# Strassen's scheme for 24 of the 32 up slabs of a decoder layer, with relu squared moved to ScalarE

## The chip, the cores and the metric

The kernel runs on one core of a Trainium2 chip. The metric is the device time of one launch in microseconds, as the median of several runs.

## What is computed

One layer of a decoder for 1056 tokens (1024 of a prompt, 32 of eight sample requests) of 1024 features: a gated convolution and pooling block, a cross attention, and a feed-forward block, each followed by a layer norm. The change lies in the last block:

```python
f = jnp.square(jax.nn.relu(x @ w1 + b1)) @ w2 + b2     # w1: 1024 x 4096, w2: 4096 x 1024
x = layer_norm(DN_ALPHA * x + f, ln3_g, ln3_b)
```

All arithmetic is in float32. For the products on TensorE each operand is kept as two parts in the matmul's own format, a high part (the rounded value) and a low part (the rest), and each product is three matmuls: high by high, high by low and low by high, all summed in PSUM.

## The kernel before, in words

Everything is held with the features on the partitions: x is 8 blocks of 128 features by 1056 tokens, as `xh` (high) and `xl` (low). A matmul writes at most a bank of PSUM, so the tokens are cut into three chunks of 384, 384 and 288 columns. The weights come as slabs of 128 partitions by 1024 columns (512 KB), one slab for one block of 128 outputs, into the two slots of `raw`.

The feed-forward block has two stages. In the **up stage** ("W1") 32 slabs of w1 are run through as plain products. GpSimd splits a slab into `wh` and `wl` (two instructions, lines 473 and 475), TensorE makes 3 chunks of 8 x 3 matmuls, ScalarE reads each chunk with bias and relu (line 1807), VectorE squares it (line 2435), and SyncE writes the finished block to `hidden` in DRAM. Slab n takes the slots of slab n-2, so its split begins when slab n-2 is done. Between the squares VectorE sets up the residual's sums in `acc` (lines 2439, 2440).

In the **down stage** ("ST") 24 of the 32 blocks of hidden values are taken by Strassen's scheme already: six groups of four blocks, each with four units of seven products of quarter size. The seven forms (sums of quarters of the hidden values, over 528 columns, half the tokens) are made by VectorE (line 2366), cast by ScalarE (line 1783) and given their low parts by VectorE and GpSimd (lines 2372, 752). The forms of the weights are made likewise for each unit: sums by VectorE (line 2388), casts by ScalarE (line 1796), low parts by GpSimd (line 759). A product is 12 matmuls of 264 columns in one of four pairs of banks, and VectorE adds it to its sums from PSUM (line 2404). The last 8 blocks are kept with both parts in DRAM and are done as plain slabs at the end ("W2").

Each engine works through a queue of its own, in the order in which the program text issues it; semaphores tie the queues together. The order is written out by hand. The first pair of up slabs is done chunk by chunk while the norm before it still writes x.

Of the kernel before, what the change touches and what calls it, by code (L numbers as in the profile page):

```python
# [6 lines left out]
P = 128  # L7
# [76 lines left out]
LATE = LAST - NU  # L84
# [27 lines left out]
STAGES += [("W1", times(16, SIX), (2, 5)), ("ST", {}, ()), ("W2", *LINEAR), ("C3", LN_MEAN, ()), ("T3", SIX, ())]  # L112
# [9 lines left out]
def decoder_step(nc, hidden, xT, memT, slabs, pool_w, params, consts, conv_state, pool_state, dec_kv,  # L122
# [76 lines left out]
    unit_high = at("unit_high", [P, 2, T], f32r, O_Q + 28 * HT * 4)  # L199
    small = at("small", [P, 80], f32, O_SMALL)  # L200
# [86 lines left out]

    def units_out(j):

        return 16 * (j // 2 + 1) + 16 * max(0, (j - KEPT) // 2 + 1)  # L290

    def squared(j):

        return 3 * j + max(0, j - KEPT)
# [8 lines left out]
    def form_order(i, G):  # L303

        by_dve = i in BY_DVE_FORMS
        order = BY_DVE_FORMS if by_dve else BY_POOL_FORMS
        return sem("form_low_dve" if by_dve else "form_low_pool"), len(order) * G + order.index(i) + 1
# [6 lines left out]
    def _(sp):  # L314
# [66 lines left out]
        def hidden_out(j):  # L381

            p = j % 2
            sp.wait_ge(sem("square"), squared(j + 1))
            block = relu[:, p, :] if j < KEPT else relu_low[:, p, :].bitcast(f32)
            sp.dma_start(hidden[:, j, :], block).then_inc(sem(f"hidden_out{p}"), 16)
            if j >= KEPT:
                sp.dma_start(hidden[:, j + NB, :], unit_high[:, p, :].bitcast(f32)).then_inc(sem(f"hidden_out{p}"), 16)

        def forms_in(G):  # L390

            b = G % 2
            if G == 0:
                for p in range(2):
                    sp.wait_ge(sem(f"hidden_out{p}"), 32)
            elif G == 1:
                sp.wait_ge(used, S_ST)
                sp.wait_ge(sem("acc_set"), NB)
                for p in range(2):
                    sp.wait_ge(sem(f"hidden_out{p}"), 64)  # L400
            else:
                sp.wait_ge(sem("st_done"), 7 * UNITS * (G - 1))
# [9 lines left out]
        for j in range(UP):  # L412
            if j < UP - 2:
                load_next(S_FF + 4 + j)
            hidden_out(j)
            if j == 9:
                forms_in(0)
        for U in range(NU):
            sp.wait_ge(sem("w_form_low"), 7 * U + 6)
            sp.wait_ge(sem("weight_sums"), 4 * (U + 1))  # L420
# [3 lines left out]
            if U >= NU - UNITS:  # L424
                if U == NU - UNITS:
                    sp.wait_ge(sem("st_done"), 7 * (NU - UNITS))
# [31 lines left out]
    def _(pool):  # L458
# [287 lines left out]
        split(S_FF + 3, 1, S_FF // 2 + 1, MEM_SLABS, freed=S_XO + 8)  # L746
        def form_low(G, i):

            f = forms_full[G % 2][:, i]
            pool.wait_ge(sem("form_sums"), 4 * (G + 1))  # L750
            pool.wait_ge(sem("form_high"), 7 * G + FORM_HIGHS.index(i) + 1)
# [3 lines left out]
        def w_form_low(U, i):  # L755

            f = 7 * U + i
            pool.wait_ge(sem("w_form_high"), f + 1)
# [3 lines left out]
        splits(S_FF + 4, S_FF + 18)  # L762
        form_low(0, 0)
        form_low(0, 4)
        splits(S_FF + 18, S_FF + 20)
        form_low(0, 5)
        form_low(0, 6)
        splits(S_FF + 20, S_ST)
# [32 lines left out]
    def _(pe):  # L801
# [465 lines left out]
        pairs("W1", S_FF, 1, UP // 2, x_parts)  # L1267

        def unit_product(U, i):
# [4 lines left out]
            pe.wait_ge(sem("w_form_low"), f + 1)  # L1274
# [81 lines left out]
    def _(act):  # L1356
# [419 lines left out]
        def form_high(G, *which):  # L1776

            for i in which:
                if i in (0, 5, 6):
                    act.wait_ge(sem("forms_in"), 64 * (G + 1))  # L1780
                else:
                    act.wait_ge(sem("form_sums"), 4 * G + {2: 1, 3: 2, 1: 3, 4: 4}[i])
                act.copy(forms_high[G % 2][:, i], forms_full[G % 2][:, i]).then_inc(sem("form_high"), 1)

        def w_form_high(U, i):

            f = 7 * U + i
            if f < 8:
                act.wait_ge(used, S_ST - 1 if f < 4 else S_ST)
            else:  # L1790
                act.wait_ge(sem("st_done"), f - 7)
            if i in (0, 4, 5):
                act.wait_ge(*unit_raw(U))
            else:
                act.wait_ge(sem("weight_sums"), 4 * U + {2: 1, 3: 2, 1: 3, 6: 4}[i])
            act.copy(wh_forms[:, f % 8, :], weight_source(U, i)).then_inc(sem("w_form_high"), 1)  # L1796

        for j in range(UP):
            p = j % 2
            if j == UP - 1:  # L1800
                for i in range(4):
                    w_form_high(0, i)
            for c, (a, z) in enumerate(CHUNKS):
                b = slab_arrived(act, "W1", S_FF + j, p, c, j // 2)
                if c == 0 and j >= 2:
                    act.wait_ge(sem(f"hidden_out{p}"), units_out(j - 2))
                act.activation(relu[:, p, a:z], ps[b][:, 0:z - a], ACT.Relu, bias=col("b1", j)).then_inc(free[b], 1)  # L1807
            if j == 14:
                form_high(0, *FORM_HIGHS)
            if j >= KEPT:  # L1810
                act.wait_ge(sem("square"), squared(j) + 3)
                act.copy(unit_high[:, p, :], relu[:, p, :]).then_inc(sem("unit_high"), 1)
# [9 lines left out]
        def late_w_high(j):  # L1822
# [3 lines left out]
            act.wait_ge(sem("st_done"), 7 * NU if j else 7 * NU - 4)  # L1826
# [55 lines left out]
    def _(dve):  # L1882
# [473 lines left out]
        def form_sums(G, *which):  # L2356
# [3 lines left out]
            for i in which:  # L2360
# [3 lines left out]
                else:  # L2364
                    dve.wait_ge(sem("form_sums"), 4 * G + {3: 1, 1: 2, 4: 3}[i])
                tt(f[:, i], f[:, x], f[:, y], op).then_inc(sem("form_sums"), 1)  # L2366

        def form_low(G, i):

            dve.wait_ge(sem("form_sums"), 4 * (G + 1))  # L2370
            dve.wait_ge(sem("form_high"), 7 * G + FORM_HIGHS.index(i) + 1)
# [3 lines left out]
        def unit_weight_sums(U, *which):  # L2375
# [3 lines left out]
            for k in which:  # L2379
                if k:  # L2380
                    dve.wait_ge(sem("weight_sums"), 4 * U + k)
                else:
                    dve.wait_ge(*unit_raw(U))
                    if U > 1:
                        dve.wait_ge(sem("w_form_low"), 7 * (U - 1))
# [4 lines left out]
        def add_product(U, i):  # L2390
# [4 lines left out]
            dve.wait_ge(sem("st_done"), 7 * U + i + 1)  # L2395
            out, y = by_banks(target), pair(7 * U + i)
            if i == 1 and U in (0, 2):
                dve.wait_ge(sem(f"hidden_out{U // 2}"), units_out(UP - 1))
# [32 lines left out]
        for j in range(UP):  # L2431
# [181 lines left out]
```

## Time and profile before

| what | us |
|---|---|
| median of 3 runs | 1381.05 |
| lowest, highest | 1379.62, 1382.85 |
| the profiled execution | 1379.41 |
| its span, first to last instruction | 1377.6 |

The up stage ends at about 1010 us of the span, the down stage with its 168 products at about 1266 us. Times in the rows below are microseconds from the span's start. The profile is of one execution. Busy time is the time in which an engine has an instruction in work; matmuls are pipelined, so the durations of single matmuls overlap and their rate has to be read from a count in a stretch.

### The profile page before, as it was taken

The numbers are of one execution on the slowest core, as the hardware profiler recorded it, in microseconds if no ns is written. First come the engines' busy times: TensorE is split into PE (matmuls) and PEld (weight loads), VectorE is DVE, ScalarE is ACT, GpSimd is POOL, SyncE is SP. The second block draws the span as 40 slices with busy tenths as digits, with TensorE's granted clock in tenths as the row PEclk, the third lists the DMA queues.
The fourth block names the chain that finished last, engine by engine and source line by source line (L and its number), as shares of the span: only waits on it lengthen the run. The fifth ranks groups of instructions, "written<-read, shape, count | busy, mean of one in ns | idle before, by whom it ended". The sixth has DMA issues, their size and how long they took to land.

```text
span 1377.6 us, 21845 instructions
## 1 busy us (share of the span) xinstructions
PE 1326.0 (96%) x8744; PEld 1279.3 (93%) x8744; DVE 882.5 (64%) x1034; ACT 431.9 (31%) x821; POOL 783.7 (57%) x576
## 2 busy tenths in 40 slices
PE   6999999999999999999999999999999999989995
PEld 6999988788899978889999999999999999989995
DVE  5899994456612762387664246324469998897767
ACT  4223442245612441145211131112243444422233
POOL 3476987544933714629433337333359999994522
PEclk9999999989999999999999999999999999999998
DMA  8222452110020266201233433333343133346112
GB/s 257 69 51 45 126 162 78 31 46 1 32 61 31 76 234 239 80 16 46 79 93 93 156 93 93 93 93 140 140 162 109 58 110 125 110 158 206 57 47 81
DMA packets 59018, 136.91 MB, mean 99 GB/s; under 512 B 21568, under 2 KB 27968, under 8 KB 56512
## 3 DMA queue, kind: packets, MB, share of 16 engines
q1 hardware_dynamic: 49184, 132.99, 29.7%
q10 hardware_dynamic: 9760, 2.93, 0.9%
q8 instruction: 47, 0.77, 0.2%
q14 instruction: 27, 0.22, 0.1%
HBM read 107.02 MB, written 28.88 MB: 99 GB/s over the span
## 4 chain that ended last, share of the span: by engine, by line
PE 62%; DVE 27%; issue 3%; POOL 3%; DMA 2%; ACT 2%; SPq 0%; DVEq 0%; ACTq 0%; POOLq 0%
PE bank L809 20%; PE bank L810 19%; PE bank L811 19%; DVE bank L1901 11%; DVE ffn_sum L2404 2%; POOL w_low L759 2%; DVE form_low L2372 1%; DVE weight_sums L2388 1%; DVE product_sums L2404 1%; DMA form_full<-hidden 1%; DVE bank L2028 1%; DVE x_full L2018 1%; DVE x_full L2035 1%; DVE form_full L2366 1%; ACT x_full L1613 1%
## 5 line engine op out<-in xcount | busy, mean ns | idle before, releaser
L809 PE MATMUL bank<-x_high,w_high 128*128 128x384 f32 (+1 forms) x1200 | 391.0, 326 | 14.5 <-POOL w_low L475 11.3
L810 PE MATMUL bank<-x_low,w_high 128*128 128x384 f32 (+1 forms) x1200 | 388.3, 324 | 0.0
L811 PE MATMUL bank<-x_high,w_low 128*128 128x384 f32 (+1 forms) x1200 | 387.6, 323 | 0.0
L809 PEld LDWEIGHTS bank<-x_high,w_high 128*128 128x128 f32 x1200 | 226.0, 188 | 17.0 <-POOL w_low L475 10.1
L473 POOL TENSOR_TENSOR w_high<-w_raw,ones 128x1024 fp32r<-128x1024 f32 x48 | 92.0, 1916 | 240.4 <-issue 128.9
L811 PEld LDWEIGHTS bank<-x_high,w_low 128*128 128x128 f32 x1200 | 226.1, 188 | 0.0
L810 PEld LDWEIGHTS bank<-x_low,w_high 128*128 128x128 f32 x1200 | 226.1, 188 | 0.0
L2435 DVE TENSOR_TENSOR relu<-relu 128x384 f32<-128x384 f32 (+1 forms) x96 | 96.6, 1010 | 187.6 <-ACT relu L1807 187.6
L809 PE MATMUL bank<-form_high,w_high 128*128 128x264 f32 x672 | 192.5, 286 | 5.1 <-DVE product_sums L2404 2.0
L810 PE MATMUL bank<-form_low,w_high 128*128 128x264 f32 x672 | 191.5, 285 | 0.0
L811 PE MATMUL bank<-form_high,w_low 128*128 128x264 f32 x672 | 190.5, 283 | 0.0
L1901 DVE SCALAR_TENSOR_TENSOR bank<-mix_full,params,bank 128x1024 f32<-128x1024 f32 x116 | 149.6, 1290 | 4.5 <-DVE mix L1928 0.5
L1807 ACT ACTIVATE relu<-bank,params 128x384 f32<-128x384 f32 (+1 forms) x96 | 53.0, 555 | 272.5 <-PE bank L811 272.5
L809 PEld LDWEIGHTS bank<-form_high,w_high 128*128 128x128 f32 x672 | 126.2, 188 | 7.4 <-DVE form_low L2372 2.8
L811 PEld LDWEIGHTS bank<-form_high,w_low 128*128 128x128 f32 x672 | 126.6, 188 | 0.0
L810 PEld LDWEIGHTS bank<-form_low,w_high 128*128 128x128 f32 x672 | 126.3, 188 | 0.0
L475 POOL TENSOR_TENSOR w_low<-w_raw,w_high 128x1024 fp32r<-128x1024 f32 x48 | 118.8, 2475 | 3.8
L759 POOL TENSOR_TENSOR w_low<-w_raw,w_high 128x256 fp32r<-128x256 f32 x96 | 92.9, 983 | 22.1 <-ACT w_high L1796 22.1
L809 PE MATMUL bank<-mix,w_high 128*128 128x384 f32 (+1 forms) x272 | 92.4, 340 | 7.9 <-DVE x_full L2312 5.0
L810 PE MATMUL bank<-mix,w_high 128*128 128x384 f32 (+1 forms) x272 | 90.8, 334 | 0.0
L811 PE MATMUL bank<-mix,w_low 128*128 128x384 f32 (+1 forms) x272 | 89.9, 331 | 0.0
L759 POOL TENSOR_TENSOR w_low<-weight_sums,w_high 128x256 fp32r<-128x256 f32 x72 | 72.7, 1021 | 22.6 <-ACT w_high L1796 22.6
(285 smaller groups left out, 2698.9 us busy)
## 6 DMA issues: line engine op xcount, KB each, us to landing
w_raw<-slabs_in SPq DMA_DIRECT2D x110, 512.0 KB, 3.7
dec_kv<-dec_kv_in SPq DMA_DIRECT2D x16, 1024.0 KB, 6.0
hidden<-relu SPq DMA_DIRECT2D x24, 528.0 KB, 5.3
form_full<-hidden SPq DMA_DIRECT2D x24, 528.0 KB, 6.6
mix<-hidden SPq DMA_DIRECT2D x16, 528.0 KB, 5.7
hidden<-relu_low SPq DMA_DIRECT2D x8, 528.0 KB, 3.9
hidden<-unit_high SPq DMA_DIRECT2D x8, 528.0 KB, 4.9
scratch<-slabs_in SPq DMA_DIRECT2D x8, 512.0 KB, 3.9
```

Of the source, the lines that this page charges most:

```text
L473: pool.tensor_tensor(high[:, slot, :], raw[:, p, :], one, ALU.mult).then_inc(high_done, 1)
L475: pool.tensor_tensor(low[:, slot, :], raw[:, p, :], high[:, slot, :].bitcast(f32), ALU.subtract).then_inc(split_done, 1)
L759: pool.tensor_tensor(wl_forms[:, f % 8, :], weight_source(U, i), wh_forms[:, f % 8, :].bitcast(f32), ALU.subtract)\
L809: pe.matmul(out, w_high, x_high, start=first, stop=False)
L810: pe.matmul(out, w_high, x_low, start=False, stop=False)
L811: return pe.matmul(out, w_low, x_high, start=False, stop=last)
L1613: act.activation(x[:, j, a:z], x[:, j, a:z], ACT.Identity, scale=col(f"ln{n}_g", j), bias=col(f"ln{n}_b", j)).then_inc(sem("x_norm"), 1)
L1807: act.activation(relu[:, p, a:z], ps[b][:, 0:z - a], ACT.Relu, bias=col("b1", j)).then_inc(free[b], 1)
L1901: return stt(out, u, w, conv_sum, ALU.mult, ALU.add)
L2018: ins = tt(x4, x4, over_blocks(ps[c][:, 0:z - a], 4), ALU.subtract)
L2404: tt(out, out, y, ALU.add).then_inc(sem("st_added"), 1)
L2435: tt(relu[:, p, a:z], relu[:, p, a:z], relu[:, p, a:z], ALU.mult).then_inc(sem("square"), 1)
```

## The change

Slabs 0 to 3 and 4 to 7 of the up stage stay plain (they are now the blocks of hidden values that are kept with both parts). The other 24 become `VU` = 12 units between them, each a pair of slabs by Strassen's scheme in Winograd's form: seven products (`UP_ORDER`) of 24 matmuls of 264 columns, with four forms of x made once (`xs_full`, `xs_high`, `xs_low`) and three sums of weights per unit (`up_weight_sums`). VectorE makes the forms of x and their low parts, ScalarE the casts; VectorE sums the products in PSUM (`up_unit`), ScalarE reads them with relu and squares them. ScalarE squares in the plain slabs too. The residual's sums move behind the 12 units and begin on ScalarE. The forms of the first down group are made during slabs 4 to 7.

TensorE:

```diff
-        pairs("W1", S_FF, 1, UP // 2, x_parts)
+        pairs("W1", S_FF, 1, 2, x_parts)
+        def up_product(f):
+            V, q = divmod(f, 7)
+            i, k = UP_ORDER[q], f % 4
+            pe.wait_ge(sem("w_form_low"), f + 1)
+            if V == 0 and i in X_FORM:
+                pe.wait_ge(sem("form_low_dve"), i)
+            if f < 4:
+                for n in (2 * k, 2 * k + 1):
+                    take(n, FREED["UP"][n])
+            else:
+                v, r = divmod(f - 4, 7)
+                if r in UP_READ:
+                    pe.wait_ge(sem("up_read"), 5 * v + UP_READ[r])
+                else:
+                    pe.wait_ge(sem("up_sums"), 7 * v + UP_SUM[r])
...
+            for c in range(2):
+                t = slice(c * HT // 2, (c + 1) * HT // 2)
+                for kb in range(4):
+                    w = slice(kb * P, (kb + 1) * P)
+                    last = product(ps[2 * k + c][:, 0:HT // 2], wh_up[:, k, w], wl_up[:, k, w], high[:, kb, t], low[:, kb, t],
+                                   kb == 0, kb == 3)
+            last.then_inc(sem("st_done"), 1)
+        for f in range(7 * VU):
+            up_product(f)
+        pe.wait_ge(sem("up_read"), 5 * VU - 1)
+        pairs("W1B", S_FF + 4, 0, 2, x_parts)
```

with `UP_ORDER = (0, 5, 1, 2, 6, 3, 4)`, `UP_READ = {0: 1, 1: 2, 3: 3, 4: 4, 6: 5}`, `UP_SUM = {2: 2, 5: 4}`.

ScalarE:

```diff
+        def up_high(f):
+            V, q = divmod(f, 7)
+            i = UP_ORDER[q]
...
+            if i in (0, 5, 4):
+                act.wait_ge(*up_raw(V, 0 if i == 0 else 1))
+            else:
+                act.wait_ge(sem("weight_sums"), 4 * V + {2: 1, 3: 2, 1: 3, 6: 4}[i])
+            act.copy(wh_up[:, f % 4, :], up_source(V, i)).then_inc(sem("w_form_high"), 1)
+        def up_relu(V, q, n, p, a):
+            act.wait_ge(sem("up_sums"), 7 * V + n)
...
+            act.activation(by_banks(y), pair(7 * V + q), ACT.Relu, bias=col("b1", 2 * V + p)).then_inc(sem("up_read"), 1)
+            act.wait_ge(sem("up_read"), 5 * V + UP_READ[q])
+            act.activation(y, y, ACT.Square).then_inc(sem("square"), 1)
+        for j in range(4):
+            up_block(j)
+            if j == 1:
+                x_high(0)
+                x_high(1)
+            if j == 2:
+                up_high(0)
+                up_high(1)
+        up_high(2)
+        up_high(3)
+        x_high(2)
+        x_high(3)
+        for f in range(7 * VU):
+            V, r = divmod(f, 7)
+            if f + 4 < 7 * VU:
+                up_high(f + 4)
+            if r == 0:
+                up_copy(V)
+            elif r == 1:
+                up_relu(V, 1, 1, 0, 0)
+            elif r == 5:
+                up_relu(V, 3, 5, 1, HT)
+                up_relu(V, 4, 6, 0, HT)
+            elif r == 6:
+                up_relu(V, 6, 7, 1, 0)
```

In the plain slabs 4 to 7 (`up_block(j)`: relu and square of each chunk, then the cast of the block) ScalarE has the seven casts of the first down group between the chunks of slab 5, two behind the first, two behind the second and three behind the third; `sum_begin(0, 1, 2, 3)` follows slab 4.

VectorE:

```diff
+        def up_unit(V):
+            d, e, g = (by_banks(up_part[:, k, :]) for k in range(3))
+            m2, m6, m5, m4, m7, m3 = (pair(7 * V + q) for q in range(1, 7))
+            dve.wait_ge(sem("up_read"), 5 * V + 1)
+            up_sum(V, 1, m2, m2, d, 2)
+            up_sum(V, 2, e, m6, d, 3)
+            up_sum(V, 3, g, m5, e, 4, 2)
+            up_sum(V, 4, e, m7, e, 6, 3)
+            up_sum(V, 5, m5, m5, e, 0, 4)
+            up_sum(V, 6, m4, m4, e, 0, 4)
+            up_sum(V, 7, m3, m3, g, 7)
+            if V + 1 < VU:
+                up_weight_sums(V + 1)
...
+        x_form(0, (l21, 1), (l22, 1), (h21, 1), (h22, 1))
+        block_low(0)
+        dve.wait_ge(sem("form_sums"), 1)
+        x_form(1, (xs_full[:, 0], 1), (h11, -1), (l11, -1))
+        block_low(1)
+        dve.wait_ge(sem("form_sums"), 2)
+        own.link(tt(xs_full[:, 3], l12, xs_full[:, 1], ALU.subtract))
+        x_low(1, 2)
+        x_low(0, 2)
+        up_weight_sums(0)
+        block_low(2)
+        x_form(2, (l11, 1), (l21, -1), (h11, 1), (h21, -1))
+        block_low(3)
+        x_low(2, 3)
+        x_form(3, (xs_full[:, 3], 1), (h12, 1))
+        x_low(3, 4)
+        for V in range(VU):
+            up_unit(V)
```

In `up_sum(V, n, out, x, y, product, needed)` the sum is `out = x + y`, behind product `product` of the unit and, where given, the sum `needed`. `up_weight_sums(V)` is four sums of 512 columns, each behind the one before; `x_form` is one sum per further term over 4 blocks of 528 columns, each behind the one before.

GpSimd:

```diff
+        for f in range(7 * VU):
+            up_low(f)
...
+        for j in range(4, NB):
+            if j < 6:
+                pool.wait_ge(sem("st_done"), 7 * VU - 2 + 2 * (j - 4))
+            split(S_FF + j, j % 2, (S_FB + j - 4) // 2, MEM_SLABS, freed=S_FF + 4 if j < 6 else S_FF + j - 1)
+            if j == 5:
+                form_low(0, 0)
+                form_low(0, 4)
+            if j == 6:
+                form_low(0, 5)
+                form_low(0, 6)
```

## Rows read from the trace of the kernel before

**Rows 1.** The page's first part: busy us, share of the span, instructions.
```profile
PE 1326.0 (96%) x8744; PEld 1279.3 (93%) x8744; DVE 882.5 (64%) x1034; ACT 431.9 (31%) x821; POOL 783.7 (57%) x576
```

**Rows 2.** Busy time by stretches: each engine's us (instructions), granted clock, DMA share, GB/s.
```profile
700.00:800.00 100.00, 100.00 (x622) 100.00 (x622) 42.21 (x38) 14.49 (x26) 36.19 (x17) 1.00 0.39 118
1100.00:1200.00 100.00, 99.27 (x811) 98.84 (x811) 89.60 (x124) 42.88 (x86) 93.48 (x80) 1.00 0.36 123
```

**Rows 3.** The timeline of GpSimd in the up stage: start, duration, instruction.
```profile
685.01 1.90 POOL L473 TENSOR_TENSOR w_high<-w_raw,ones 128x1024 fp32r<-128x1024 f32 x1 [7.14 <-issue]
686.99 2.48 POOL L475 TENSOR_TENSOR w_low<-w_raw,w_high 128x1024 fp32r<-128x1024 f32 x1
696.64 1.90 POOL L473 TENSOR_TENSOR w_high<-w_raw,ones 128x1024 fp32r<-128x1024 f32 x1 [7.17 <-PE bank L811]
```

**Rows 4.** The timeline of VectorE and ScalarE before the down stage, weight sums and casts.
```profile
1002.93 0.42 DVE L2388 TENSOR_TENSOR w_raw<-w_raw 128x256 f32<-128x256 f32 x1
1003.38 0.43 DVE L2388 TENSOR_TENSOR weight_sums<-w_raw 128x256 f32<-128x256 f32 x1
...
1003.90 0.71 ACT L1796 CAST w_high<-weight_sums 128x256 fp32r<-128x256 f32 x2 [2.87 <-DVE weight_sums L2388]
```

**Rows 5.** One line's instructions each: count, ns min/median/max, first and last start.
```profile
L2404 DVE TENSOR_TENSOR ffn_sum<-ffn_sum,bank x96: 687/692/706, 1014.8 to 1264.5; 128x528 f32<-128x528 f32 x96
L2366 DVE TENSOR_TENSOR form_full<-form_full x24: 1243/1253/3439, 803.3 to 1203.3; 128x1056 f32<-128x1056 f32 x24
L1796 ACT CAST w_high<-w_raw x96: 397/406/412, 1000.6 to 1251.1; 128x256 fp32r<-128x256 f32 x96
L1783 ACT CAST form_high<-form_full x42: 1064/1076/1081, 813.1 to 1204.6; 128x1056 fp32r<-128x1056 f32 x42
L1807 ACT ACTIVATE relu<-bank,params x96: 501/582/586, 655.1 to 1010.2; 128x384 f32<-128x384 f32 x64, 128x288 f32<-128x288 f32 x32
```

**Rows 6.** The timeline where a chunk ends: the next chunk's first matmul, its relu.
```profile
688.90 0.34 PE L809 MATMUL bank<-x_high,w_high 128*128 128x384 f32 x1
...
689.10 0.58 ACT L1807 ACTIVATE relu<-bank,params 128x384 f32<-128x384 f32 x1 [3.72 <-PE bank L811]
```

**Rows 7.** Stretches around three pauses of TensorE, columns as in rows 2.
```profile
623.00:624.00 1.00, 0.00 (x0) 0.00 (x0) 1.00 (x2) 1.00 (x3) 1.00 (x2) 1.00 0.00 0
625.00:630.00 5.00, 5.00 (x26) 5.00 (x27) 4.12 (x5) 0.89 (x2) 4.05 (x4) 0.66 0.00 0
...
192.00:196.00 4.00, 3.95 (x12) 3.03 (x13) 3.90 (x4) 0.00 (x0) 4.00 (x3) 0.61 0.63 151
214.00:218.00 4.00, 2.10 (x13) 1.93 (x13) 2.57 (x5) 3.53 (x8) 3.40 (x2) 1.00 0.47 131
218.00:222.00 4.00, 4.00 (x28) 4.00 (x27) 1.11 (x2) 1.37 (x1) 3.31 (x2) 1.00 0.91 327
```

**Rows 8.** The timeline at the up stage's start: GpSimd, VectorE twice, ScalarE.
```profile
651.17 6.51 POOL L675 TENSOR_TENSOR x_low<-x_full,x_high 128x288 fp32r<-128x288 f32 x8
...
660.09 2.91 DVE L2439 TENSOR_SCALAR ffn_sum<-x_high,params 128x1056 f32<-128x1056 f32 x1
665.51 0.77 DVE L2439 TENSOR_SCALAR ffn_sum<-x_high,params 128x1056 f32<-128x1056 f32 x1
...
661.64 0.51 ACT L1807 ACTIVATE relu<-bank,params 128x288 f32<-128x288 f32 x1 [1.75 <-PE bank L811]
```

**Rows 9.** DMA issues in the page's sixth part: count, KB each, median us to landing.
```profile
w_raw<-slabs_in SPq DMA_DIRECT2D x110, 512.0 KB, 3.7
...
hidden<-relu SPq DMA_DIRECT2D x24, 528.0 KB, 5.3
form_full<-hidden SPq DMA_DIRECT2D x24, 528.0 KB, 6.6
```

More of the change, by code:

```diff
@@ L383, in hidden_out, with pair_out @@
             p = j % 2
[L384 to L388, printed above, removed]
+            sp.wait_ge(sem("block_low"), j + 1)
+            sp.dma_start(hidden[:, KEPT + j, :], relu_low[:, p, :].bitcast(f32)).then_inc(sem(f"hidden_out{p}"), 16)
+            sp.dma_start(hidden[:, UP + j, :], block_high(j).bitcast(f32)).then_inc(sem(f"hidden_out{p}"), 16)
+        def pair_out(V):
+            for p, n in ((0, 3), (1, 4)):
+                sp.wait_ge(sem("square"), squared(4) - 4 * VU + 4 * V + n)
+                sp.dma_start(hidden[:, 2 * V + p, :], relu[:, p, :]).then_inc(sem(f"hidden_out{p}"), 16)
         def forms_in(G):
@@ L1801, in _ @@
+        for j in range(4, NB):
+            if j == NB - 1:
                 for i in range(4):
                     w_form_high(0, i)
[L1803 to L1809, printed above, removed]
@@ L1810, in _ @@
[L1810 to L1812 removed]
+            up_block(j)
+            if j == 4:
+                act.wait_ge(sem("w_form_low"), 7 * VU)
+                act.wait_ge(sem("up_sums"), 7 * VU)
+                sum_begin(0, 1, 2, 3)
+            if j == 5:
+                sum_begin(4, 5, 6, 7)
         for U in range(NU):
@@ new lines, in up_sum @@
+        def up_sum(V, n, out, x, y, product, needed=0):
+            if product:
+                dve.wait_ge(sem("st_done"), 7 * V + product)
+            if needed:
+                dve.wait_ge(sem("up_sums"), 7 * V + needed)
+            tt(out, x, y, ALU.add).then_inc(sem("up_sums"), 1)
+        def up_unit(V):
[11 more added lines that the diff above has]
+                up_weight_sums(V + 1)
@@ new lines, in sum_set, with x_form @@
+        def sum_set(j):
+            dve.wait_ge(sem("sum_begun"), j + 1)
+            ins = stt(acc[:, j, :], xl[:, j, :].bitcast(f32), ALPHA, acc[:, j, :], ALU.mult, ALU.add)
+            if j >= UNITS:
+                own.link(ins)
+                ins = tt(acc[:, j, 0:HT], acc[:, j, 0:HT], acc[:, j, HT:T], ALU.subtract)
+            ins.then_inc(sem("acc_set"), 1)
+        def x_form(k, *terms):
+            out, (x, op) = xs_full[:, k], terms[0]
+            for n, (y, sign) in enumerate(terms[1:]):
+                ins = tt(out, x, y, ALU.add if sign > 0 else ALU.subtract)
+                x = out
+                if n < len(terms) - 2:
+                    own.link(ins)
+            ins.then_inc(sem("form_sums"), 1)
```

211 lines of the change are left out of this document (146 added, 65 removed).

## The prediction

> **What bounds the kernel now.** I read the shares first. TensorE is busy for 96% of the span, VectorE for 64%, ScalarE for 31% [rows 1]. Then the same by stretches: in the up stage (700 to 800 us) and the down stage (1100 to 1200 us) TensorE has 100.0 and 99.3 us of work in 100, at full clock [rows 2]. So both stages cost what TensorE's instructions cost; the other engines are hidden. The up stage runs at one slab in 11.63 us, read from GpSimd, which splits slab n the moment slab n-2 is done (685.01, 696.64) [rows 3]. Less TensorE work is therefore worth its full time there, as long as nobody lets TensorE wait. That second half decides here.
>
> **1. The products.** Twenty-four slabs go, 24 x 11.63 = 279.1 us. In come 12 units (pairs of slabs) of 7 products, each of 2 chunks x 4 blocks x 3 = 24 matmuls of 264 columns. The down stage runs the same matmul: 99.27 us / 811 = 0.1224 us each [rows 2]. A product is 2.94 us, a unit 20.6, all 84 are 246.8. Gain: **-32.3 us**.
>
> **2. The seam between two units.** Seven products share four pairs of banks, so product f may start only when the pair of product f-4 is read. The first product of unit V+1 needs the fourth of unit V (q = 3) read, which is `up_relu(V, 3, ...)` on ScalarE. In ScalarE's queue the step f = 7V+5 issues `up_high(7V+9)` ahead of that relu. `up_high(7V+9)` is the cast for form 1 of unit V+1, and form 1 is the third weight sum of that unit. VectorE's `up_unit(V)` issues the next unit's weight sums at its end, behind `up_sum(V, 7)`, which waits for the last product of unit V. Queued behind the waiting cast are both relus (q = 3, 4); TensorE waits for the first of them. So from the end of unit V nothing overlaps any longer:
> - hand-over TensorE to reader 0.2 us (chunk over at 688.90, relu starts 689.10) [rows 6];
> - `up_sum` 7 over 528 columns in PSUM 0.69 (L2404) [rows 5];
> - three dependent weight sums of 512 columns. 256 columns take 0.42 [rows 4] and 1056 take 1.25 (L2366) [rows 5], in between lies 0.68; with 0.04 from one to the next (1002.93 + 0.42 to 1003.38) [rows 4] that is 3 x 0.72 = 2.16;
> - the cast of 512 columns, between 0.406 (256) and 1.076 (1056) [rows 5]: 0.62;
> - the relu of 528 columns, 0.58 for 384 (L1807) [rows 5] and 0.84 ns for each further column by the two casts: 0.70;
> - two more hand-overs (1003.81 to 1003.90 in rows 4; to TensorE no row, taken as the 0.2 above): 0.3.
>
> Together 4.6 us. Low end 4.0 (operations overlap at their ends), high end 5.6 (one VectorE sum held up by a GpSimd operation of about 1.3 us). Eleven seams: **+50.6** (44 to 62). Within a unit I find no stall: a cast, a low part on GpSimd (512 columns, against 2.48 us for 1024 [rows 3]) and the reads of PSUM all have at least one product of 2.94 us of lead, and a slab lands in 3.7 us [rows 9]. The squares move to ScalarE at no cost: it works some 12 us a unit.
>
> **3. The start: forms of x.** Before the low parts of the first forms are done VectorE can add up nothing. It starts at 657.7, when the last low parts of x are written (651.17 + 6.51) [rows 8]. Its queue: ten sums, four low parts (each over 2112 columns, 2.4 us by 1.25 x 2 minus a start [rows 5]), four block low parts of 1.25, and four weight sums; 42 us. GpSimd's operations come on top: a VectorE operation that meets one waits for its end; the same operation took 2.91 us at 660.09 beside GpSimd and 0.77 at 665.51 without [rows 8]. I add the two rest splits (4.4) and four 512-column low parts (5). Two waits for ScalarE add about 2. The last two forms thus come late: `x_form(2)` ends near 700, ScalarE casts it, `x_form(3)` and its cast end near 709.5. On ScalarE `up_high(4)` is queued behind these casts, so w_low for product 4 is there near 711. TensorE finishes blocks 2, 3 at 685 (slab 1 is done at 661.6 [rows 8], and 2 x 11.63 on) and four products at 697. **+13** (9 to 15).
>
> **4. The way out.** After product 83 TensorE waits for `up_relu(11, 4)`: three PSUM sums and three ScalarE operations from the end of product 82, about 3.9 us against one product of 2.94: **+1** (0 to 2). Then four full slabs, 4 to 7. Call their start T. GpSimd's queue for slab 5 is split(5), form_low(0, 0), form_low(0, 4), and only then split(6). form_low(0, 4) waits for the last of the seven casts of the down forms, and ScalarE does the last three behind the third chunk of block 5, which ends at T + 23.3: relu and square 1.0, catch-up 2, three casts of 1.0. So form_low(0, 4) runs from T + 29.4, 2.6 long, split(6) takes 1.90 + 2.48 [rows 3], and slab 6 is ready at T + 36.5 to 37.5 where TensorE wants it at T + 23.3. **+13.5** (10 to 16). The forms themselves (out 5.3 us, back 6.6 us [rows 9]) land at about T + 17, before that matters. The kernel before has this order too, but splits two slabs ahead and casts in one go.
>
> **5. The clock.** After a pause the granted clock can fall to its lower level, 1.2 GHz. TensorE rests through 623 to 624, and over 625 to 630 the granted clock is 0.66 in the mean, which is 3.4 us at half rate; over 192 to 196 it is 0.61, right behind another pause; the pause inside 214 to 218 has 1.00 in it and behind it [rows 7]. One fall of 3.4 us costs 1.7 us. The pauses here (4.6 and 13 us) are longer than each of these. I take a fall for each of 13, at 1.4 us since part of it lies in the pause: **+18** (0 to 26). The Trainium skill (TensorE: Matmul & The Clock Gate, Part 1) says that the throttled clock is the default and that activity releases it. By that rule no long pause goes free, which is the third case below; the row at 214 to 218 shows that a short one can.
>
> **Sum.** -32.3 + 50.6 + 13 + 1 + 13.5 + 18 = +63.8 us. The profiled execution took 1379.41 us (span 1377.6), so 1443.2; the median of the three runs lies 1.64 above it: 1445 us. Everything behind slab 7 stays as it is: forms, their low parts and the first weight sums are done before T + 59.
>
> **Rivals.**
> - *Forecast*: seams of 4.6 us and most falls of the clock, 1445 us. Chance 0.62.
> - *The clock holds* through the seams, as behind 214 us: 18 less, 1427 us. For it: the seam leaves 20 of 25 us busy. Against: at 625 TensorE had been busy until shortly before its pause, and the clock fell. 0.18.
> - *More than counted*: all falls in full (26) and VectorE's sums held up by GpSimd at seams (62): 1379.4 - 32.3 + 62 + 13 + 1 + 13.5 + 26 = 1462.6, with the offset 1464. Against: at the seam GpSimd has nothing ready to do. 0.13.
> - *TensorE stays fed* (the other side). It would be so if the weight sums of the next unit ran before `up_sum(V, 7)` or if the relus were not behind the cast; then the seams cost nothing, and neither do their falls. It decides from a seam under (32.3 - 13 - 1 - 13.5) / 11 = 0.4 us. With the pauses of parts 3 and 4 left it gives 1376 us, with these hidden too 1349. Against: both orders are written out in the queues, and nothing but chance timing could undo them. 0.05.
> - Mixtures near zero: 0.02.
>
> Range: the low end takes no falls and the low ends of all pauses, -32.3 + 44 + 9 + 0 + 10 = +31, 1412; the high end the high ends, 1470. A measurement of this kernel tells 0.2% (2.8 us) from no change. Faster 0.05, same 0.02, slower 0.93; predicted 1445.
>
> **What would show it.** Eleven pauses of TensorE of 4 to 5 us, 25 to 27 us apart, each ended by the relu of q = 3 on ScalarE; ahead of it ScalarE waiting for `up_weight_sums`, VectorE busy in a row from the last product on. One pause of about 13 us near 700 us, ended by GpSimd's low part of a weight, and one of about 13 us in front of slab 6, ended by GpSimd's split. Matmuls of 264 columns 0.122 us apart in between. Granted clock under 1 in a good part of the slices of the stage. It is wrong if the seams are under 1 us, if TensorE waits inside the units, or if products take other than 2.94 us.

## The result, and the profile after the change

The changed kernel is slower by 5.9%: 1463.0 us in the median (1460.5 to 1465.1, 4 runs) beside 1381.8 us for the kernel before, ratio 1.0589 with a 95% interval of 1.0567 to 1.0611. Its profiled span is 1461.7 us, 84.1 more than before.

Three lines of the page after, to set beside [rows 1]: busy time of TensorE and its loads, of VectorE, ScalarE and GpSimd, and then the 40 slices of TensorE and its granted clock.

```profile
PE 1330.5 (91%) x9032; PEld 1279.4 (88%) x9032; DVE 894.3 (61%) x1076; ACT 536.1 (37%) x977; POOL 795.4 (54%) x612
...
PE   6999989998999999999588888888699999999996
...
PEclk9999999899999999999799899899889999999998
```

TensorE was busy for 96% of the span and is for 91% now. Its busy time did not fall but rose a little (1326.0 to 1330.5 us), though the matmuls cover fewer columns. In the slices the up stage stands out as one row of eights, between a five and a six, and the clock beneath it is no longer even. The waits of the stretch from 690 to 1100 us (engine and line, whom it waited for: us in total, times, longest) name the cause:

```profile
PE bank L873 <- ACT relu L1944: 47.7, 12, 4.3
PE bank L873 <- POOL w_low L802: 13.4, 1, 13.4
PE bank L873 <- POOL w_low L526: 13.4, 1, 13.4
PE bank L873 <- ACT relu L1899: 1.9, 1, 1.9
...
ACT w_high L1929 <- DVE up_weight_sums L2627: 86.5, 11, 8.1
```

In words: twelve waits for the relu of the units (L1944: eleven seams of 4.25 us and the way out, 0.91), one of 13.4 us for the low part of product 4's weights (L802), one of 13.4 us for the split of slab 6 (L526), and one of 1.9 us ahead of the down stage's first product (L1899). ScalarE in turn waited eleven times for VectorE's weight sums. One seam in order of time, VectorE, ScalarE, TensorE (start, duration, instruction):

```profile
884.50 0.72 DVE L2635 TENSOR_TENSOR bank<-bank,up_parts 128x528 f32<-128x528 f32 x1 [0.84 <-PE bank L875]
885.12 0.68 DVE L2627 TENSOR_TENSOR up_weight_sums<-w_raw 128x512 f32<-128x512 f32 x1
885.84 0.69 DVE L2627 TENSOR_TENSOR w_raw<-w_raw 128x512 f32<-128x512 f32 x1
886.56 0.69 DVE L2627 TENSOR_TENSOR up_weight_sums<-w_raw 128x512 f32<-128x512 f32 x1
...
887.35 0.62 ACT L1929 CAST w_high<-up_weight_sums 128x512 fp32r<-128x512 f32 x1 [8.07 <-DVE up_weight_sums L2627]
887.87 0.69 ACT L1944 ACTIVATE relu<-bank,params 128x528 f32<-128x528 f32 x1
...
884.18 0.28 PE L875 MATMUL bank<-x_form_high,w_low 128*128 128x264 f32 x1
888.71 0.56 PE L873 MATMUL bank<-x_high,w_high 128*128 128x264 f32 x1 [4.25 <-ACT relu L1944]
```

The unit's last matmul ends at 884.46; then one sum of products, three weight sums, one cast and one relu run one behind the other, each starting within 0.1 us of the end of the one before, and at 888.71, 0.15 us behind the relu, TensorE begins again. The relu itself was ready to run from about 883.0 on, when the fifth sum had ended (the fifth and the sixth run from 882.33 to 883.66); it stood behind the cast.

After the pause comes the clock. The stretches around the same seam (us, busy time of the five engines, granted clock, DMA share, GB/s; clock third from last):

```profile
886.00:888.00 2.00, 0.00 (x0) 0.00 (x0) 1.92 (x3) 0.65 (x2) 0.00 (x0) 0.81 0.00 0
889.00:894.00 5.00, 5.00 (x24) 5.00 (x24) 0.00 (x0) 3.23 (x6) 1.59 (x2) 0.50 0.44 182
894.00:900.00 6.00, 6.00 (x51) 6.00 (x51) 0.72 (x1) 3.09 (x5) 2.57 (x2) 1.00 0.08 31
```

24 matmuls in 5 us at 1.2 GHz against 51 in 6 us at 2.4 GHz. The clock had already fallen in the pause (0.81 over 886 to 888) and came back at about 894.1. The unit ahead of this seam shows the price: its 168 matmuls took 23.06 us (861.40 to 884.46), where seven products at full clock take 20.4 (experiment 1), so 5.35 us at half rate cost 2.7.

The start and the way out. First ScalarE, VectorE and GpSimd ahead of product 4:

```profile
698.74 1.95 ACT L1915 CAST x_form_high<-x_form_full 128x2112 fp32r<-128x2112 f32 x1 [9.73 <-DVE x_form_full L2665]
705.38 1.95 ACT L1915 CAST x_form_high<-x_form_full 128x2112 fp32r<-128x2112 f32 x1 [4.69 <-DVE x_form_full L2665]
707.24 0.61 ACT L1929 CAST w_high<-up_weight_sums 128x512 fp32r<-128x512 f32 x1
...
703.00 2.35 DVE L2665 TENSOR_TENSOR x_form_full<-x_form_full,x_high 128x2112 f32<-128x2112 f32 x1
...
707.93 2.92 POOL L802 TENSOR_TENSOR w_low<-up_weight_sums,w_high 128x512 fp32r<-128x512 f32 x1 [13.83 <-ACT w_high L1929]
```

Then GpSimd around slabs 6 and 7:

```profile
1042.40 3.42 POOL L813 TENSOR_TENSOR form_low<-form_full,form_high 128x1056 fp32r<-128x1056 f32 x1 [16.83 <-DVE form_full L2537]
1050.07 2.42 POOL L813 TENSOR_TENSOR form_low<-form_full,form_high 128x1056 fp32r<-128x1056 f32 x1 [4.24 <-ACT form_high L1877]
1052.45 2.90 POOL L524 TENSOR_TENSOR w_high<-w_raw,ones 128x1024 fp32r<-128x1024 f32 x1
1055.43 3.23 POOL L526 TENSOR_TENSOR w_low<-w_raw,w_high 128x1024 fp32r<-128x1024 f32 x1
```

The split of slab 6 begins at 1052.45, behind a low part that waited for ScalarE's cast, while TensorE had been idle from 1045.4.

**The account of the 84.1 us.** Products: 84 x 2.91 us, by the rate of the first experiment below, for 24 x 11.63 us [rows 3], -34.5. Pauses in the stage: 11 x 4.25 + 13.4 + 0.9 + 13.4 = 74.5, and two of 1.9 at the down stage's start, 78.3 together. Low clock while TensorE worked: behind nine seams 5.35 us each, behind the first two seams 3.4 us each, 5.7 and 5.9 us behind the two long pauses, twice 3.4 at the down stage; half of the 73.4 us is 36.7. The sum is +80.5, and 3.6 us are left. Of these 1.3 lie ahead of the change (a pause of TensorE that began at 616.48 us begins at 617.79; in the other runs of the changed kernel it begins anywhere from 616.6 to 620.2) and 1.4 behind TensorE's last pause (13.9 us to the end of the span before, 15.3 after); 0.9 us isn't assigned.

### The profile page after: what moved, and what is told of

The parts are those of the page before. It is cut to its first block, busy times and chain, and to the rows that moved or that the text cites. A ratio compares the mean times of both kernels' runs of the same rounds, so it can differ in the third digit from the quotient of the medians.

```text
span 1461.7 us, 22709 instructions
## 1 busy us (share of the span) xinstructions
PE 1330.5 (91%) x9032; PEld 1279.4 (88%) x9032; DVE 894.3 (61%) x1076; ACT 536.1 (37%) x977; POOL 795.4 (54%) x612
## 3 DMA queue, kind: packets, MB, share of 16 engines
q1 hardware_dynamic: 49184, 132.99, 26.4%
## 4 chain that ended last, share of the span: by engine, by line
PE 50%; DVE 30%; POOL 6%; issue 5%; ACT 5%; DMA 4%; SPq 0%; DVEq 0%; ACTq 0%; POOLq 0%
PE bank L873 16%; PE bank L874 15%; PE bank L875 15%; DVE bank L2072 10%; DVE ffn_sum L2575 2%; DVE x_form_full L2665 2%; DVE form_low L2543 2%; DMA form_full<-hidden 2%; DVE weight_sums L2559 1%; POOL w_low L820 1%; POOL x_low L726 1%; DVE up_weight_sums L2627 1%; DMA w_raw<-slabs_in 1%; DVE product_sums L2575 1%; ACT x_full L1707 1%
## 5 line engine op out<-in xcount | busy, mean ns | idle before, releaser
L873 PE MATMUL bank<-x_high,w_high 128*128 128x384 f32 (+2 forms) x912 | 301.4, 330 | 89.1 <-ACT relu L1944 47.7
L874 PE MATMUL bank<-x_low,w_high 128*128 128x384 f32 (+2 forms) x912 | 297.5, 326 | 0.0
L875 PE MATMUL bank<-x_high,w_low 128*128 128x384 f32 (+2 forms) x912 | 296.5, 325 | 0.0
L875 PEld LDWEIGHTS bank<-x_high,w_low 128*128 128x128 f32 x912 | 185.7, 204 | 0.0
L802 POOL TENSOR_TENSOR w_low<-up_weight_sums,w_high 128x512 fp32r<-128x512 f32 x36 | 50.7, 1408 | 141.9 <-ACT w_high L1929 141.9
L802 POOL TENSOR_TENSOR w_low<-w_raw,w_high 128x512 fp32r<-128x512 f32 x48 | 63.5, 1325 | 90.3 <-ACT w_high L1929 90.3
L873 PE MATMUL bank<-x_form_high,w_high 128*128 128x264 f32 x384 | 109.3, 285 | 0.0
L875 PE MATMUL bank<-x_form_high,w_low 128*128 128x264 f32 x384 | 109.0, 284 | 0.0
L874 PE MATMUL bank<-x_form_low,w_high 128*128 128x264 f32 x384 | 109.0, 284 | 0.0
L2635 DVE TENSOR_TENSOR bank<-bank,up_parts 128x528 f32<-128x528 f32 x48 | 33.2, 714 | 111.2 <-PE bank L875 110.8
L873 PE MATMUL bank<-mix,w_high 128*128 128x384 f32 (+1 forms) x272 | 92.3, 339 | 6.4 <-DVE x_full L2483 3.5
L2635 DVE TENSOR_TENSOR up_parts<-bank,up_parts 128x528 f32<-128x528 f32 x36 | 25.5, 708 | 111.9 <-PE bank L875 111.8
```

The source lines that it names most:

```text
L802: pool.tensor_tensor(wl_up[:, f % 4, :], up_source(f // 7, UP_ORDER[f % 7]), wh_up[:, f % 4, :].bitcast(f32), ALU.subtract)\
L873: pe.matmul(out, w_high, x_high, start=first, stop=False)
L874: pe.matmul(out, w_high, x_low, start=False, stop=False)
L875: return pe.matmul(out, w_low, x_high, start=False, stop=last)
L2635: tt(out, x, y, ALU.add).then_inc(sem("up_sums"), 1)
```

## The experiments

The theory: TensorE's pauses are made by three orders written into the queues (the relus behind the cast that waits for weight sums; the weight cast of product 4 behind those of the forms; the split of slab 6 behind low parts), and the clock falls because of the pauses. All ratios are to the kernel before.

**1. The relus ahead of the cast** (changed kernel, ScalarE's loop):

```diff
+            if r == 5:
+                up_relu(V, 3, 5, 1, HT)
+                up_relu(V, 4, 6, 0, HT)
             if f + 4 < 7 * VU:
                 up_high(f + 4)
...
-            elif r == 5:
-                up_relu(V, 3, 5, 1, HT)
-                up_relu(V, 4, 6, 0, HT)
```

> Changed kernel, with the two relus of products q = 3 and 4 issued on ScalarE ahead of the cast of form 1 of the next unit; nothing else moved. Theory (the relu stands behind a cast that waits for VectorE's weight sums, and the falls of the clock follow from these pauses): the eleven pauses of 4.25 us go to under 0.3 us each, because the relu of q = 3 ends 2.4 us after the sixth product and the seventh takes 2.9; the cast and its low part are ready 5 us after the unit's end, and product q = 2 wants them at 5.9. 47 us of pauses and some 26 us of low clock go: 1463 - 73 = 1390 us. Rival 1 (the weight sums themselves are late for TensorE, whatever ScalarE's order): the pause moves to product q = 2 and keeps 2 to 4 us: 1420 to 1440. Rival 2 (the clock is low for another reason than the pauses): 1463 - 47 = 1416, with the low stretches still there.

Measured: 1386.3 us, ratio 1.0024 (1.0013 to 1.0035). The eleven seams are gone, and with them every low stretch of the clock between 720 and 940 us; the line of that stretch is

```profile
720.00:940.00 220.00, 220.00 (x1813) 220.00 (x1812) 82.61 (x121) 106.05 (x175) 96.63 (x76) 1.00 0.29 105
```

220 us of work in 220 us at full clock, 1813 matmuls, 0.1213 us each: the product takes 2.91 us, and the gain that the change is made for is real. Moving two lines gave back 76.7 us of 81. Both rivals fall: no pause moved to product q = 2, and the low clock went with the pauses.

**2. The weight sums ahead of the fourth sum** (changed kernel, VectorE's `up_unit`; ScalarE's order left as it is):

```diff
             up_sum(V, 3, g, m5, e, 4, 2)
+            if V + 1 < VU:
+                up_weight_sums(V + 1)
             up_sum(V, 4, e, m7, e, 6, 3)
...
             up_sum(V, 7, m3, m3, g, 7)
-            if V + 1 < VU:
-                up_weight_sums(V + 1)
```

> Changed kernel, with the next unit's four weight sums issued on VectorE ahead of the fourth sum of products, where VectorE waits for the sixth product anyway; ScalarE's order is as in the change. Theory: either half of the chain is enough. The second slab half of the next unit lands some 16 us after the unit's start, the sums are done by about 19, the cast of form 1 follows the sixth product (17.6) at once, and the relu of q = 3 ends near 20.5 where the seventh product ends: pauses of 0 to 0.8 us, 1390 to 1400 us. Rival (the order on ScalarE alone makes the pause, the place of the sums on VectorE doesn't matter): pauses stay near 4.25 us and the time at 1463.

Measured: 1394.7 us, ratio 1.0085 (1.0059 to 1.0111). TensorE's wait for the relus nearly goes:

```profile
PE bank L873 <- ACT relu L1944: 4.6, 4, 2.5
```

Four waits, 4.6 us in all. So it was enough to break either half of the chain, as expected; the pause of 4.25 us needs both orders. This half alone leaves a little: a pause of 2.5 us at the first seam, and 8.4 us more in the median than experiment 1.

**3. Matmuls into the seams** (changed kernel, TensorE, ahead of the first product of units 1 to 11):

```diff
+            if V and q == 0:
+                pe.wait_ge(sem("up_sums"), 7 * V - 3)
+                for n in range(32):
+                    pe.matmul(ps[2 * ((f - 2) % 4) + n % 2][:, 0:264], wh_up[:, k, 0:P], xh[:, n % 8, 0:264], start=True, stop=True)
```

> Changed kernel, with 32 matmuls of 264 columns more in each of the eleven seams, into a free pair of banks; their results are overwritten. The order of all else is as in the change. They take 3.9 us of each seam of 4.25. Theory (the pauses lower the clock, and that costs time of its own): the granted clock stays at full through the units, and the 5.4 us at half rate behind a seam come back as 2.7 us: 9 x 2.7 + 2 x 1.7 = 27 us, 1436 us, with the seams as long as before from product to product. Rival (the low clock costs nothing, since the units wait for others then): 1463. Rival 2 (the fillers' reads and writes slow VectorE and ScalarE in the seam): over 1463.

Measured: 1431.9 us, ratio 1.0358 (1.0332 to 1.0385), 31 us less than the changed kernel for 352 matmuls more. The added matmuls of one seam and the clock of a stretch that holds one:

```profile
896.07 4.06 PE L1341 MATMUL bank<-x_high,w_high 128*128 128x264 f32 x32
...
900.00:910.00 10.00, 9.74 (x81) 9.61 (x80) 1.26 (x2) 7.50 (x13) 4.98 (x4) 1.00 0.30 118
```

From 717 us to the end of the units the granted clock is 1.00. The seams are about as long as before (4.1 us of filler and 0.3 of pause), so what went in the units is the price of the clock alone. By the two profiles, whose spans are 30.1 us apart, 25.4 us of it lie in the units (from product 4's first matmul to the last product's end, 310.1 us in the changed kernel and 284.7 here), where the low stretches behind the seams add up to 27.5. Most of the rest lies behind the units: the two pauses of 1.9 us around the down stage's first products are there in this run too, but the granted clock stays at 1.00 behind them. It is a test, not a remedy; it shows that the falls in the units come from TensorE's idleness and cost time of their own.

**4 and 5. The split of slab 6, and then of slabs 6 and 7, ahead of the low parts** (changed kernel, GpSimd; the run with one split has `j == 6` in the place of `j == 7`):

```diff
-            if j == 5:
-                form_low(0, 0)
-                form_low(0, 4)
-            if j == 6:
-                form_low(0, 5)
-                form_low(0, 6)
+            if j == 7:
+                for i in BY_POOL_FORMS:
+                    form_low(0, i)
```

> Changed kernel, with GpSimd's split of plain slab 6 issued ahead of the four low parts of the first down forms instead of behind two of them. Theory: the 13.4 us pause ahead of slab 6 is that order alone; the split then ends at about 16 us of the 23 us that slabs 4 and 5 take. The pause goes, and 3.0 us of low clock with it: 1463 - 16 = 1447 us. Rival (the forms are late for the down stage, and the pause only stood ahead of that): the low parts come later now, the down stage's first product waits for them, and 3 us or less are left of the gain: 1460.

Measured: 1451.6 us, ratio 1.0505 (1.0476 to 1.0535). The expected 16 us became 11: the pause ahead of slab 6 was gone, and 8.8 us of it stood ahead of slab 7, whose split was now behind all four low parts. I had looked at one slab only.

> Changed kernel, with GpSimd's splits of plain slabs 6 and 7 both ahead of all four low parts of the first down forms. With slab 6's split alone ahead, the pause of 13.4 us moved to slab 7 and kept 8.8 us, as the low parts then stood ahead of split 7. Theory: with both ahead nothing of it is left, and the low parts, some 10 to 14 us of work from the end of slab 5 on, are done before the down stage asks: no pause over 1 us ahead of slabs 6 and 7; 8.8 us and 1 to 3 us of low clock less than with one split ahead, 1440 us against 1463 of the change. Rival: the low parts are late now, the down stage's first products wait, and 2 to 8 us of it stand there: 1445 to 1452.

Measured: 1453.3 us, ratio 1.0526 (1.0508 to 1.0543), no better. TensorE's wait had moved again:

```profile
PE bank L870 <- ACT relu L1896: 9.0, 1, 9.0
...
ACT w_high L1887 <- DVE weight_sums L2556: 17.9, 1, 17.9
```

Now ScalarE stood for 17.9 us at a cast for the down stage, with the relus of slab 7 behind it, and waited for VectorE's weight sums. VectorE was far behind, since it and GpSimd held each other up. In that run:

```profile
1053.06 10.43 DVE L2652 SCALAR_TENSOR_TENSOR ffn_sum<-x_low,ffn_sum 128x1056 f32<-128x1056 f32 x3
...
1051.98 13.84 POOL L813 TENSOR_TENSOR form_low<-form_full,form_high 128x1056 fp32r<-128x1056 f32 x4
```

Three sums of the residual took 10.4 us beside four low parts that took 13.8; alone they are 1.25 and 2.4 us each. The rival (the forms' low parts are late) is nearer than my theory of one order, but what was late were the residual's sums and the weight sums queued behind them.

**6. The way out lightened.** As the run with both splits, and three of the residual's eight sums (blocks 0, 3, 4) are made in the units, where VectorE idles; the first weight sums and the low parts stand ahead of the others. The main lines:

```diff
+EARLY, SUM_ORDER = {1: 0, 2: 3, 3: 4}, (0, 3, 4, 1, 2, 5, 6, 7)
...
         for V in range(VU):
             up_unit(V)
+            if V - 1 in EARLY:
+                sum_set(EARLY[V - 1])
...
+            if j == 6:
+                unit_weight_sums(0, 0, 1, 2, 3)
+                form_low(0, BY_DVE_FORMS[1])
+                form_low(0, BY_DVE_FORMS[2])
+            for b in ((1, 2), (5,), (6, 7), ())[j - 4]:
+                sum_set(b)
```

> The run with both splits ahead (1453 us, where 9.0 us of pause were left in front of the down stage), with VectorE's queue behind the units lightened and reordered: the residual's sums of blocks 0, 3 and 4 are made between units 2, 3 and 4, and the first weight sums and the low parts of the down forms stand ahead of the other residual's sums. Theory (the way out is bound by VectorE and GpSimd, which wait for each other: five sums of 1.25 us alone took 10.4 and 2.9 there, and four low parts 13.8): 6 to 8 us of VectorE's work leave the stretch and the rest of the sums hide in the down stage's first unit; the pause of 9.0 goes to 0 to 2, and the three sums in the units add nothing there, as VectorE waits over half of each: 1453 - 10 = 1443 us. Rival (the forms' way through DRAM and ScalarE's seven casts bound it): the pause keeps 6 us or more, 1450.

Measured: 1450.5 us, ratio 1.0499 (1.0478 to 1.0519). The pause fell from 9.0 to 6.0 us and is ended by VectorE's copy of a product's sums. Direction right, size a third of what I had expected: the rival's bound of 6 us is what came, though by VectorE and not by ScalarE.

**7. Fewer sums for the forms of x** (changed kernel, VectorE; leaves the low parts of x out of the forms, five of ten sums):

```diff
-        x_form(0, (l21, 1), (l22, 1), (h21, 1), (h22, 1))
+        x_form(0, (h21, 1), (h22, 1))
...
-        x_form(1, (xs_full[:, 0], 1), (h11, -1), (l11, -1))
+        x_form(1, (xs_full[:, 0], 1), (h11, -1))
...
-        x_form(2, (l11, 1), (l21, -1), (h11, 1), (h21, -1))
+        x_form(2, (h11, 1), (h21, -1))
```

> Changed kernel, with the low parts of x left out of the forms' sums (five of the ten sums of 2112 columns go; the forms' values are slightly off by that). Theory (the 13.4 us pause at product 4 is VectorE's queue): four of the five sums stand ahead of the third form or in it, 2.4 us each on the path, up to 1 us more where GpSimd's work stood in their way: the pause falls by 10 to 13 us, to 0 to 3.5 us, and 3 us of low clock go: 1463 - 14 = 1449 us. Rival (the pause hangs on ScalarE, which comes to the forms' casts only behind blocks 2 and 3, and on slab loads): it falls by 5 us or less: 1457 or more.

Measured: 1453.7 us, ratio 1.0532 (1.0511 to 1.0551); the pause at product 4 went from 13.4 to 4.2 us:

```profile
PE bank L873 <- POOL w_low L802: 4.2, 1, 4.2
```

So work in VectorE's queue makes at least 9.2 us of the 13.4. That is a little under the 10 to 13 expected for five sums of 2.4 us; what holds the last 4.2 us wasn't tested.

**8. The start reordered, nothing left out** (changed kernel). ScalarE:

```diff
         x_high(2)
+        up_high(4)
+        up_copy(0)
+        up_high(5)
+        up_relu(0, 1, 1, 0, 0)
         x_high(3)
-        for f in range(7 * VU):
+        for f in range(2, 7 * VU):
```

and VectorE makes `up_sum` 1 and 2 of unit 0 ahead of `x_form(3, ...)`.

> Changed kernel, with nothing left out, but reordered at the start: ScalarE casts the weights of products 4 and 5 and reads the first products ahead of the cast of the last form of x, and VectorE makes the first two sums of products ahead of that form. Theory (product 4 waits only because its weight cast stands behind the casts of forms that it doesn't use): product 4 starts without a pause at 697.5, product 5 at about 703.5 when the third form's low part is there, product 6 at about 711.5. The first unit ends near 715 in place of 722.5: 1456 us. Rival (VectorE's queue bounds all three alike): product 6 is later than 713 and the time stays over 1460.

Measured: 1458.3 us, ratio 1.0553 (1.053 to 1.0575), 4.7 us less than the change. Product 4 did wait, from 697.0 to 703.7, as `up_high(4)` was still behind the cast of the third form, which I had overlooked:

```profile
698.20 1.95 ACT L1915 CAST x_form_high<-x_form_full 128x2112 fp32r<-128x2112 f32 x1 [9.75 <-DVE x_form_full L2667]
700.06 0.61 ACT L1929 CAST w_high<-up_weight_sums 128x512 fp32r<-128x512 f32 x1
```

Product 5 came at 708.2 (expected 703.5), product 6 at 712.7 (expected 711.5), and the first unit ended at 715.9 in place of 722.5. Nearly 1 us of that went again, as the first seam was 5.2 us in place of 4.25. Its line shows why: one weight sum took 1.63 us in place of 0.69, beside a low part of GpSimd whose cast had waited for a slab half (6.1 us, to 716.26).

```profile
717.25 1.63 DVE L2631 TENSOR_TENSOR w_raw<-w_raw 128x512 f32<-128x512 f32 x1
...
716.96 1.38 POOL L802 TENSOR_TENSOR w_low<-w_raw,w_high 128x512 fp32r<-128x512 f32 x1 [3.08 <-ACT w_high L1929]
```

So the theory failed at product 4 and was close from product 6 on. The new order took 6.6 us off product 4's pause; experiment 7 took 9.2 off the same pause in another way, so the 13.4 us are not one engine's alone.

**9. The squares alone** (the kernel before, with relu squared on ScalarE):

```diff
                 act.activation(relu[:, p, a:z], ps[b][:, 0:z - a], ACT.Relu, bias=col("b1", j)).then_inc(free[b], 1)
+                act.wait_ge(free[b], FREED["W1"][b] + j // 2 + 1)
+                if c == 0 and j:
+                    act.wait_ge(sem("square"), squared(j))
+                act.activation(relu[:, p, a:z], relu[:, p, a:z], ACT.Square).then_inc(sem("square"), 1)
```

> The kernel before, with the squares of all 32 up blocks moved from VectorE to ScalarE and nothing else of the change. Theory: that part costs and gains nothing, as it is done by an engine that works 15 of 100 us there: 1382 us, within 0.2% of before. Rival 1 (ScalarE's squares delay its reads of PSUM or need a table of its own loaded again and again, 1.3 us each): 3 us or more slower. Rival 2 (VectorE was in somebody's way through the port that it shares with GpSimd): 3 us or more faster.

Measured: 1381.1 us, ratio 0.9994 (0.9982 to 1.0006). In the plain slabs that part of the change is worth nothing and costs nothing. The table that rival 1 spoke of isn't loaded again either: the last ACT_TABLE_LOAD of this trace is at 596.8 us, ahead of the up stage.

**10 to 12. All orders together.** The relus first, both splits first, the start's order, and the down stage's first weight sums ahead of the residual's last sums:

> Changed kernel with five orders put right and nothing left out: the relus of q = 3 and 4 ahead of the cast, both splits ahead of the low parts, the start's order as in the run on it, and the first weight sums of the down stage ahead of the residual's last sums. Theory (pauses and low clock were the whole loss, and the 84 products of 2.92 us gain 34 us): 1386.3 with the relus moved, less 13.4 and 3 us for slabs 6 and 7, less 7 us at the start, less 2 us ahead of the down stage: 1361 us, ratio 0.985 to the kernel before. Rival (the parts hide each other: without one pause the next engine is late, as where the split of slab 6 alone was moved): 1370 or more.

Measured: 1374.4 us, ratio 0.9947 (0.993 to 0.9963). Faster than the kernel before, but 13 us short of the forecast: the rival held. 9.5 us of pause stood ahead of the down stage's second product, ended by VectorE. With the residual's three sums moved into the units:

> All orders put right as in the run before (1374.4 us), and the residual's sums moved as in the run beside this one. Theory: the 9.5 us ahead of the down stage's second product go, with 2 to 3 us of low clock: 1363 us, ratio 0.986 to the kernel before. Rival (without a pause at the seams the units have no room for the three sums on ScalarE and VectorE, and pauses of 1 to 2 us come back there): 1368 or more.

Measured: 1371.5 us, ratio 0.9927 (0.991 to 0.9943), 8 us short of the forecast. The time is in the rival's range, but not for the rival's reason: the units had room (behind the first seam there is no pause among them), and 6.0 us were left at the way out, ended by VectorE. With a fourth sum moved (that of block 5; the buffer `up_part` lies 768 bytes further on to make room):

> The run before (1371.5 us, with 6.0 us of pause in front of the down stage, ended by VectorE), with the residual's sum of block 5 made behind unit 5 too, and those of blocks 6 and 7 one slab earlier each. Theory (VectorE's queue bounds the way out): one block's two sums leave the stretch, 2.0 us alone and up to 6.4 beside GpSimd; the pause falls from 6.0 to 1 to 4 us, 1366 to 1369 us. Rival (ScalarE or GpSimd bounds it): the pause stays between 5 and 7, 1371.

Measured: 1369.2 us, ratio 0.9909 (0.9892 to 0.9925). The waits of TensorE from 690 to 1030 us that are left in it:

```profile
PE bank L871 <- POOL w_low L803: 8.1, 2, 6.7
PE bank L871 <- DVE product_sums L2577: 4.5, 1, 4.5
PE bank L871 <- ACT relu L1942: 2.5, 2, 1.6
```

The pause at the way out went from 6.0 to 4.5 us for one block's sums, just outside the 1 to 4 expected, and is ended by VectorE each time. The longest pause left is the one at product 4, 6.7 us. This is the fastest version measured: 13 us under the kernel before, 94 under the change.

## Why the prediction was right, and where not

It said slower, 1445 us in a range of 1412 to 1470; it came to 1463. Step by step:

- *The products* (-32.3): right. 2.91 us measured where 2.94 stood, -34.5. The rate came from a stretch of the down stage [rows 2] with a count, and held for products twice as long.
- *The seams* (+50.6): right in place, chain and number (eleven), 4.25 us each for 4.6. Each link has its counterpart: sum 0.72 for 0.69, weight sums 0.68 to 0.69 for 0.68, cast 0.62 for 0.62, relu 0.69 for 0.70. The links as listed add up to 4.67, not 4.6. Of the 0.42 too much, 0.2 lies in the overlap of independent neighbours (the first weight sum and the relu each begin 0.1 us before the end of the one ahead), which was left for the low end, and 0.16 in the first hand-over (0.04 us, 884.46 to 884.50, for 0.2). Experiments 1 and 2 show both orders to be needed.
- *The start* (+13): 13.4. Experiment 7 shows work in VectorE's queue for 9.2 of it; experiment 8, with the cast of product 4's weights ahead of the last form's, shows the orders named in the prediction for 6.6. The two overlap.
- *The way out* (+1 and +13.5): 0.9 and 13.4. The order on GpSimd made the pause in the form it had, as predicted. What I hadn't seen is that it was one of several that lay under each other: VectorE, with the residual's sums, was nearly as late (experiments 4 to 6). And the sentence that everything behind slab 7 stays as it is was wrong by two pauses of 1.9 us.
- *The clock* (+18): the term that was mis-sized. It came to 36.7 by the trace; the high end of 26 was too low. I had taken one stretch of 3.4 us behind each pause [rows 7], partly hidden in the pause. Nine of eleven seams had 6.8 us at 1.2 GHz behind them, 5.35 of it while TensorE worked, 2.7 us each. In the changed kernel's profile every pause of 1.9 us or more from product 4 to the down stage had such a stretch behind it, but the length of a pause doesn't settle it: in experiments 1 and 3 the same two pauses of 1.9 us had none. Experiment 3 shows the part of the term that lies in the units, 25 us by the profiles. The rule of the Trainium skill (TensorE: Matmul & The Clock Gate, Part 1) that idle gaps cost clock as well as time was on the right side; by the trace they cost twice what I had put for them.

The miss of 18 us is about that term, +18.7. The others nearly cancel: products -2.2, seams -3.8, the two pauses at the down stage +3.8, +3.6 outside the account's terms, and -2 for the place of the profiled execution among its runs (1.6 us under the median of the earlier runs, 0.4 over it now).

The third rival's number, 1464, lies closer to the result than the forecast, but that is luck: it had seams of 62 us in all, held up by GpSimd, where 46.8 came, and 26 us for the clock, where 36.7 came.

## What to carry to other kernels

When a consumer is queued behind a producer's cast on an in-order engine, follow the cast to what it waits for: two independent orders made a chain here that cost 77 of the 81 us, and putting either one right took nearly all of it away (76.7 us for one, 68.3 for the other). Price a periodic pause of TensorE with the clock behind it, not by its length alone: eleven pauses of 4.25 us cost 77 us here, 7 each. And when a pause is ended by one engine's order, look at how late the next engine is before counting on the gain.

## What the runs showed of the hardware

- Seams of 4.25 us, 26.4 to 27.3 us apart, in the changed kernel: behind the first two the granted clock was at 1.2 GHz for 3.4 us, around and behind the other nine for 6.8 us. The same seams, as long as these, came out otherwise in another run: in experiment 6 it was 6.8 us at all eleven. With the seams filled with matmuls there was no fall.
- Two pauses of 1.9 us, 14 us apart, were each followed by 3.4 us at 1.2 GHz in the changed kernel (1086.4 and 1100.3 us) and by none in experiments 1 and 3 (granted clock 1.00 from 991 to 1372 us in experiment 1).
- An operation of VectorE with two inputs from SBUF and one of GpSimd lengthen each other in turn: three scalar-tensor-tensor operations of 1.25 us took 10.4 us beside four low parts of 2.4 us, which took 13.8. VectorE's sums from PSUM stayed at 0.70 to 0.72 us (all 84 of L2635 in the changed kernel), also where one ran wholly beside a low part of GpSimd (at 709.64 us). In [rows 8] only the one-input form had shown that. The run with both splits has it for a single operation too, 3.45 us at 1036.06 us where 1.26 is its time alone. The Trainium skill (SBUF — State Buffer, "SBUF: two separate sides") says that the two engines share a pair of ports under a lock and counts operations with two SBUF inputs among the cases; the trace agrees, by these numbers.
